# RWKV-7 outputs turned to channels by tokens, with centred values as weights and their squares summed on TensorE

## The chip, the cores and the metric
One core of one Trainium2 chip. The metric is device time in microseconds of one execution of the whole program. The kernel before: 929.25 us, median of 3 runs (929.19 to 930.19). Engines are named as in the profile: PE (TensorE), DVE (VectorE), ACT (ScalarE), POOL (GpSimd), SP (the queue that issues most loads).

## The reference
A two-layer trunk over 256 tokens of width 1024: an RWKV-7 time mix, a SwiGLU block, a shared K/V projection, a dilated window attention and a second SwiGLU block. Only the output of the time mix is touched. Cut to what matters:

```python
o = wkv7_scan(rh, decay, kh, vh, -kk, kk * ah)     # (1, 256, 16 heads, 64), linear in vh
mean = jnp.mean(o, axis=-1, keepdims=True)         # per token and head
var = jnp.mean(jnp.square(o - mean), axis=-1, keepdims=True)
o = (o - mean) * lax.rsqrt(var + LNX_EPS)
o = o.reshape(Bn, Sn, Dn) * lnx_g + lnx_b
bonus = jnp.sum(rh * kh * r_k, axis=-1, keepdims=True) * vh
y = (o + bonus.reshape(Bn, Sn, Dn)) * g            # then y @ w_o, added to x
```

The scan is linear in the values, so values whose mean over the 64 channels of a head has been taken away give outputs whose mean is already zero.

## The kernel before
The time mix runs as four groups (`group(it)`, it 0 to 3) of 256 channels, that is four heads; the program is written out by hand for each engine, with semaphores between them, so that each engine's order is the order of the code. In a group the 256 tokens are two chunks of 128. The stages of a group on PE, in order:

- the head: `second_rank` (two small products), the query projection in four quarters (`project_parts(4, ...)`), `turn_output(it)` (the outputs of the group before are turned by four transposes into bank 2), `sums_of_squares` (squares of the keys), the value projection (`values`) with `turn_norms` (L650 to 654) inside it;
- the matrices (`pe_mats`), with `product_o` of the group before between the chunks;
- six levels `l` of a blocked triangular inverse, small matmuls that alternate with DVE; `values_fill(l)` puts other work of PE between them. At `l == 4` it turns the values `vT` by four transposes (L741) into `Vn`, tokens by channels;
- the state phase (L786 to 848): the last products of the inverse, then for chunk 0 `UUs`, the new state (`pe_S`, bank 2), the output (`pe_o`, bank 3), for chunk 1 `pe_z1`, `UUs`, and the output (bank 6). `next_keys(v)` puts a quarter of the next group's key projection between them; the last group has none, and `keep_clock` multiplies the identity by itself there.

The outputs of a group lie tokens by channels. DVE's `norm_output(it, c)` takes the sum over the 64 channels of a head, subtracts the mean, ACT squares (`square_output`), DVE sums the squares, POOL takes the root (`root`, L2123), DVE scales into `on`. `turn_output` then turns `on`, and `gate_turned` (or `gate_output` at the end) multiplies by the gain and the gate, adds the bonus, and the product with `w_o` follows. `pe_on`, `dve_on`, `dve_oc`, `act_osq`, `pool_ors` are the semaphores of this chain.

After the last group comes a tail (L864 to 870): `product_o(NGRP, [0])`, the turn of chunk 1, `product_o(NGRP, [1], 1, [0])`, `turn_half_rows(0, 0)` (the normalised first token tile of the SwiGLU block, which needs both halves of `product_o` of tile 0 added to x), `product_o(NGRP, [1], 1, [1])`. Most matmuls are recorded at the helper's line L496, transposes at their own line. A matmul of plain float32 shows as two records of weight load and matmul, a transpose as one.

Of the kernel before, what the change touches and what calls it, by code (L numbers as in the profile page):

```python
# [16 lines left out]
ALU = mybir.AluOpType  # L17
# [24 lines left out]
def constants():  # L42
# [4 lines left out]
    out["halves"] = (p // HD == f // HD).astype(np.float32)  # L47
    strict, incl = (p < f), (p <= f)
# [40 lines left out]
def program(nc, ins, out):  # L89
    ctx = ExitStack()  # L90
    with ctx:
# [51 lines left out]
        ident, halves = C("ident"), C("halves")  # L143
# [82 lines left out]
        on = cg.take(512, "p (c n i) -> p c n i", c=2, n=2)  # L226
        yT = cg.take(512, "p (n t) -> p n t", n=2)
# [266 lines left out]
        def _(pe):  # L494
# [135 lines left out]
            def group(it, behind=True, ahead=True):  # L630


                def next_keys(v):
# [6 lines left out]
                    else:  # L640
# [17 lines left out]
                if behind:  # L658
# [3 lines left out]
                    turn_output(it)  # L662
# [46 lines left out]
                def values_fill(l):  # L709
# [112 lines left out]
                pe.wait_ge(S("dve_S"), it + 1)  # L822
                pe.wait_ge(S("pool_M"), it * 2 + 2)
                for n in range(2):
                    mm(bank[4][:, n * P:(n + 1) * P], ar[:, n, 1, 0, :], St[:, n, :], True, False)
                    for h in range(2):
                        u = 2 * n + h
                        m = mm(hcols(bank[4], u), M[:, 4 + u, 2, :], Vn[:, 1, n, h * HD:(h + 1) * HD], False, h == 1)
                m.then_inc(S("pe_z1"), 1)
                next_keys(2)  # L830
# [9 lines left out]
                for n in range(2):  # L840
                    mm(bank[6][:, n * P:(n + 1) * P], ar[:, n, 1, 1, :], St[:, n, :], True, False)
                    for h in range(2):
                        u = 2 * n + h
                        hh = slice(h * HD, (h + 1) * HD)
                        o = hcols(bank[6], u)
                        mm(o, M[:, 4 + u, 3, :], Vn[:, 1, n, hh], False, False)
                        m = mm(o, M[:, 4 + u, 1, :], UUs[:, 1, n, hh], False, h == 1)
                m.then_inc(S("pe_o"), 1)
# [260 lines left out]
        def _(act):  # L1109
# [65 lines left out]
            def square_output(it, c):  # L1175
                act.wait_ge(S("dve_oc"), it * 2 + (c - 1))
                A(osq[:, c * T:(c + 1) * T], oc[:, c * T:(c + 1) * T], ACT.Square).then_inc(S("act_osq"), 1)

            def group(it, behind=True, ahead=True):
# [38 lines left out]
                if behind:  # L1218
                    decays()
                else:  # L1220
# [62 lines left out]
                for c in range(2):  # L1283
                    if c == 1 and not ahead:
                        square_output(NGRP, 0)
                    if c == 1:
                        act.wait_ge(S("pe_z1"), it + 1)
# [6 lines left out]
                if ahead:  # L1294
                    A(small[:, 63:64], onec[:, 0:1], ACT.Sigmoid)
                    square_output(it + 1, 0)
# [4 lines left out]
            square_output(NGRP, 1)  # L1301

# [200 lines left out]
        def _(dve):  # L1503
# [143 lines left out]
            def norm_output(it, c, meanwhile=None, squaring=None):  # L1647

                o = bank[(3, 6)[c]][:, 0:T].rearrange("p (u i) -> p u i", u=4)
                cut = slice(c * T, (c + 1) * T)  # L1650
                st = [gsm[:, 8 * i + 4 * c:8 * i + 4 * c + 4] for i in range(6)]
                dve.wait_ge(S("pe_o"), it * 2 + (c - 1))
# [544 lines left out]
```

## Time and profile before

| | before |
|---|---|
| median of 3 runs | 929.25 us (929.19 to 930.19) |
| the profiled execution's own time | 934.33 us |
| its span | 932.0 us |
| mean granted TensorE clock | 0.993 |
| busy: PE, DVE, ACT, POOL | 920.8, 681.7, 501.8, 101.4 us |
| the time mix in the span | about the first 273 us |

The profiled execution is 5.08 us longer than the median of the runs. Times in the trace count from the start of its span. PE's busy time counts a matmul until its modelled end, so the pace of PE is read from starts, not from busy shares.

### The profile page before, as it was taken

How to read it: one execution, taken by the hardware profiler on the slowest of the kernel's cores; microseconds unless marked ns; L12 is line 12 of the kernel's file. 1: busy time of each engine (PE TensorE's matmuls, PEld its weight loads, DVE VectorE, ACT ScalarE, POOL GpSimd, SP SyncE). 2: the span in 40 equal slices, each digit the busy share in tenths (PEclk: the TensorE clock that was granted, in tenths of full speed). 3: DMA queues.
4: the chain of work that ended last, by engine and by line, in shares of the span. 5: the costliest groups of instructions: out<-in, count | busy, mean ns of one | idle time of the engine just before them, and what ended most of it. 6: DMA issues, size and time to landing. Idle time of an engine off the chain costs nothing.

```text
span 932.0 us, 18317 instructions
## 1 busy us (share of the span) xinstructions
PE 920.8 (99%) x7008; PEld 818.6 (88%) x7008; DVE 681.7 (73%) x1294; ACT 501.8 (54%) x818; POOL 101.4 (11%) x75
## 2 busy tenths in 40 slices
PE   9999999999999999999999999999999999999998
PEld 7789889798879888888899999999998888888887
DVE  7877877778466756666687888889879666666665
ACT  4563544544244545444457776767777445445442
POOL 0211000000012000000041133213222000000000
PEclk9999999999799999999999999999999999999999
DMA  9311213203407676667369545554654256676661
GB/s 298 132 60 46 91 60 105 92 1 107 145 1 202 178 223 178 185 193 217 104 206 292 152 132 163 148 155 139 171 159 114 71 162 186 192 203 195 188 180 45
DMA packets 195241, 136.71 MB, mean 147 GB/s; under 512 B 7390, under 2 KB 186078, under 8 KB 195180
## 3 DMA queue, kind: packets, MB, share of 16 engines
q1 hardware_dynamic: 194748, 135.13, 49.3%
q8 instruction: 44, 0.72, 0.3%
q10 hardware_dynamic: 432, 0.72, 0.3%
q14 instruction: 17, 0.14, 0.1%
HBM read 134.78 MB, written 1.05 MB: 146 GB/s over the span
## 4 chain that ended last, share of the span: by engine, by line
PE 94%; DVE 3%; issue 2%; ACT 1%; POOL 0%; POOLq 0%; DVEq 0%
PE bank L496 52%; PE wide L496 37%; DVE work L1505 1%; PE wide L1029 1%; PE wide L1052 1%; PE bank L1029 1%; PE bank L1052 1%; DVE x L1505 0%; POOL gsm L2123 0%; PE wide L653 0%; PE wide L741 0%; PE wide L787 0%; PE bank L519 0%; ACT work L1111 0%; PE bank L596 0%
## 5 line engine op out<-in xcount | busy, mean ns | idle before, releaser
L496 PE MATMUL bank<-wpj,hkq 128*128 128x384 f32 x1152 | 215.5, 340 | 1.5 <-ACT Vs L1111 0.4
L496 PEld LDWEIGHTS bank<-wpj,hkq 128*128 128x128 f32 x1152 | 197.5, 188 | 6.1 <-issue 4.2
L496 PE MATMUL wide<-hsp,wsp 128*128 128x256 f32 (+2 forms) x1120 | 196.0, 329 | 1.6 <-DVE hsp L1505 1.6
L496 PEld LDWEIGHTS wide<-hsp,wsp 128*128 128x128 f32 x1120 | 172.4, 190 | 24.3 <-DVE hsp L1505 2.4
L1505 DVE TENSOR_TENSOR wsp<-ring,wsp 128x1024 fp32r<-128x1024 f32 (+1 forms) x88 | 150.6, 1752 | 4.2 <-ACT wsp L1111 4.2
L1111 ACT ACTIVATE wsp<-ring 128x1024 fp32r<-128x1024 f32 (+1 forms) x88 | 130.3, 1484 | 26.5 <-DMA ring<-in_f_w_gu 15.6
L2123 POOL TENSOR_TENSOR gsm<-gsm,mhalf 128x6 f32<-128x6 f32 (+1 forms) x40 | 74.3, 1876 | 317.4 <-DVE gsm L2041 174.0
L1111 ACT ACTIVATE rows<-wide 128x256 f32<-128x256 f32 x66 | 25.4, 384 | 145.7 <-PE wide L496 145.7
L496 PE MATMUL bank<-wsp,asp 128*128 128x512 f32 x396 | 98.1, 392 | 0.0
L1505 DVE TENSOR_TENSOR wpj<-ring,wpj 128x1536 fp32r<-128x1536 f32 x48 | 84.1, 1753 | 17.0 <-ACT wpj L1111 17.0
L496 PEld LDWEIGHTS bank<-wsp,asp 128*128 128x128 f32 x396 | 71.8, 189 | 13.1
L1111 ACT ACTIVATE wpj<-ring 128x1536 fp32r<-128x1536 f32 x48 | 71.1, 1485 | 6.6 <-PE bank L496 6.3
L496 PEld LDWEIGHTS bank<-work 64*64 64x64 f32 (+4 forms) x1216 | 58.9, 140 | 16.1 <-issue 6.2
L496 PE MATMUL bank<-work 64*64 64x32 f32 (+7 forms) x1216 | 71.1, 237 | 1.6
L1505 DVE TENSOR_TENSOR am<-sg,rows 128x256 f32<-128x256 f32 x44 | 19.1, 435 | 71.4 <-ACT sg L1111 70.8
L496 PE MATMUL bank<-hsp,wsp 128*128 128x256 f32 (+1 forms) x368 | 68.7, 330 | 0.0
L1111 ACT ACTIVATE work<-wide 128x256 f32<-128x256 f32 (+3 forms) x73 | 30.9, 441 | 67.6 <-PE wide L496 28.6
L496 PE MATMUL wide<-work 64*64 64x32 f32 (+6 forms) x720 | 62.7, 265 | 0.7 <-DVE work L1505 0.4
L496 PEld LDWEIGHTS bank<-hsp,wsp 128*128 128x128 f32 x368 | 56.9, 190 | 6.2
L496 PEld LDWEIGHTS wide<-work 64*64 64x64 f32 (+4 forms) x720 | 54.4, 160 | 4.5 <-issue 1.7
L1505 DVE TENSOR_TENSOR rows<-wide,rows 128x256 f32<-128x256 f32 x66 | 27.9, 424 | 37.3 <-ACT rows L1111 37.3
L496 PE MATMUL wide<-wsp,asp 128*128 128x512 f32 x132 | 37.1, 390 | 0.0
(295 smaller groups left out, 1333.4 us busy)
## 6 DMA issues: line engine op xcount, KB each, us to landing
ring<-in_f_w_gu SPq DMA_DIRECT2D x88, 512.0 KB, 6.0
ring<-in_w_kv SPq DMA_DIRECT2D x96, 256.0 KB, 3.5
ring<-in_f_w_down SPq DMA_DIRECT2D x44, 512.0 KB, 3.7
ring<-in_b_w_q SPq DMA_DIRECT2D x48, 256.0 KB, 3.4
wmix<-in_a_w_k SPq DMA_DIRECT2D x4, 1024.0 KB, 5.2
wmix<-in_a_w_r SPq DMA_DIRECT2D x4, 1024.0 KB, 5.6
wmix<-in_a_w_v SPq DMA_DIRECT2D x4, 1024.0 KB, 5.3
wmix<-in_a_w_o SPq DMA_DIRECT2D x4, 1024.0 KB, 5.0
```

The source lines that it names most:

```text
L496: return pe.matmul(o, a, b, start=start, stop=stop)
L1029: m = pe.transpose(QK[w][r][:, g * P:(g + 1) * P], akr[:, 2 * w + r, g * P:(g + 1) * P], ident)
L1052: m = pe.transpose(SCORES[r][h][:, j * P:(j + 1) * P], pr[r][:, h, j * P:(j + 1) * P], ident)
L1111: return act.activation(o, i, f, **k)
L1505: return dve.tensor_tensor(o, a, b, op)
L2123: return pool.tensor_tensor(dst, src, mhalf[:, 0:n], ALU.pow)
```

## The change
- The outputs are computed channels by tokens. `heads_out` makes four matmuls, for two pairs n and two heads h: the weights are 64 columns of the values (`Vn`), of `UUs` or of the state `St`, 128 tokens of a matrix M or `ar` move, and head h lands in its own 64 partitions of bank 3 or 6. Before, M (128 columns) was the weight and 64 channels moved.
- `vT` is turned by four float32 matmuls with the constant `centre` (identity less 1/64 within a head) instead of by four transposes, so that `Vn` is centred.
- ACT squares the outputs straight from the banks. PE sums the squares of each head with `output_squares` (two matmuls a chunk, two columns moving), in front of `sums_of_squares`. DVE makes the variance for both chunks in one step, POOL takes one root of 8 columns, ACT spreads it (`spread_roots`) into `on`, and `turn_output` turns that into bank 1, now between quarters 1 and 2 of `values`.
- DVE: `norm_output` goes; `gate_heads` multiplies the outputs by gain and gate straight from banks 3 and 6; one multiplication with the turned roots is put ahead of `dve_scaled`.
- The state phase: the products with `Vn` and M are put ahead of the waits for `act_uu` and `dve_S`.
- The last group: `keep_clock` stays for v 0 and 2 alone; the turn of chunk 0 leaves the state phase; the tail is reordered.

The core of the diff:

```diff
+    out["centre"] = out["ident"] - out["halves"] / HD
@@ turn_output, output_squares
-                pe.wait_ge(S("dve_on"), it * 2 + (chunks[-1] - 1))
+                pe.wait_ge(S("act_ors"), it + (chunks[-1] if it == NGRP else 0))
...
+            def output_squares(it, c, b):
+                pe.wait_ge(S("act_osq"), it * 2 + (c - 1))
+                for n in range(2):
+                    m = mm(bank[b][:, 8 + 4 * c + 2 * n:10 + 4 * c + 2 * n], osq[:, c * T + n * P:c * T + (n + 1) * P], halves[:, 0:P:HD])
+                return m
@@ head of a group on PE
-                        keep_clock((4, 4, 4, 3)[v], 7)
+                    elif v in (0, 2):
+                        keep_clock(4, (7, 1)[v // 2])
...
                     pe.wait_ge(S("act_sq"), it + 1)
+                    if behind:
+                        pe.wait_ge(S("dve_oc"), it * 2)
+                        for c in range(2):
+                            output_squares(it, c, 3)
...
-                    turn_output(it)
                     sums_of_squares()
...
-                    values(range(early - 1, 4))
+                    values([early - 1])
                     pe.wait_ge(S("act_sa"), it + 1)
+                    turn_output(it, b=1)
+                    values(range(early, 4))
@@ values_fill, l == 4
-                                m = pe.transpose(bank[6][:, (2 * c + n) * P:(2 * c + n + 1) * P],
-                                                 vT[:, n * T + c * P:n * T + (c + 1) * P], ident)
+                                m = mm(bank[6][:, (2 * c + n) * P:(2 * c + n + 1) * P], vT[:, n * T + c * P:n * T + (c + 1) * P], cent)
@@ state phase
+                def heads_out(b, c, first, weights, moving, last):
+                    for n in range(2):
+                        for h, hh in enumerate(BLK):
+                            m = mm(bank[b][hh, n * P:(n + 1) * P], weights(n, hh), moving(n, 2 * n + h), first and n == 0, last and n == 1)
+                    return m
+                for n in range(2):
+                    mm(bank[2][:, n * P:(n + 1) * P], kPn[:, n, :], Vn[:, 0, n, :], n == 0, False)
+                pe.wait_ge(S("act_U"), it * 2 + 2)
+                heads_out(3, 0, True, lambda n, hh: Vn[:, 0, n, hh], lambda n, u: M[:, u, 3, :], False)
                 pe.wait_ge(S("act_uu"), it * 2 + 1)
                 for n in range(2):
-                    mm(bank[2][:, n * P:(n + 1) * P], kPn[:, n, :], Vn[:, 0, n, :], True, False)
-                    m = mm(bank[2][:, n * P:(n + 1) * P], bPn[:, n, :], UUs[:, 0, n, :], False, True)
+                    m = mm(bank[2][:, n * P:(n + 1) * P], bPn[:, n, :], UUs[:, 0, n, :], False, n == 1)
                 m.then_inc(S("pe_S"), 1)
+                heads_out(3, 0, False, lambda n, hh: UUs[:, 0, n, hh], lambda n, u: M[:, u, 1, :], True).then_inc(S("pe_o"), 1)
+                pe.wait_ge(S("pool_M"), it * 2 + 2)
                 for u in range(4):
-                    hh = slice((u % 2) * HD, (u % 2 + 1) * HD)
-                    mm(hcols(bank[3], u), M[:, u, 3, :], Vn[:, 0, u // 2, hh], True, False)
-                    m = mm(hcols(bank[3], u), M[:, u, 1, :], UUs[:, 0, u // 2, hh], False, True)
-                m.then_inc(S("pe_o"), 1)
+                    mm(hcols(bank[4], u), M[:, 4 + u, 2, :], Vn[:, 1, u // 2, (u % 2) * HD:(u % 2 + 1) * HD], u == 0, False)
...
                 m.then_inc(S("pe_z1"), 1)
+                if not ahead:
+                    output_squares(NGRP, 0, 7).then_inc(S("pe_ss"), 1)
                 next_keys(2)
...
+                heads_out(6, 1, True, lambda n, hh: St[:, n, hh], lambda n, u: ar[:, n, 1, 1, :], False)
+                heads_out(6, 1, False, lambda n, hh: Vn[:, 1, n, hh], lambda n, u: M[:, 4 + u, 3, :], False)
                 next_keys(3)
-                if not ahead:
-                    turn_output(NGRP, [0])
                 pe.wait_ge(S("act_uu"), it * 2 + 2)
...
+                heads_out(6, 1, False, lambda n, hh: UUs[:, 1, n, hh], lambda n, u: M[:, 4 + u, 1, :], True).then_inc(S("pe_o"), 1)
@@ tail on PE
-            product_o(NGRP, [0])
-            keep_clock(1, 4)
+            turn_output(NGRP, [0])
+            keep_clock(2, 4)
+            output_squares(NGRP, 1, 7).then_inc(S("pe_ss"), 1)
+            product_o(NGRP, [0], 0, [0])
+            pe.wait_ge(S("dve_oc"), NGRP * 2 - 1)
             turn_output(NGRP, [1], 3)
-            keep_clock(6, 4)
+            product_o(NGRP, [0], 0, [1])
+            keep_clock(2, 4)
             product_o(NGRP, [1], 1, [0])
@@ ACT
-                act.wait_ge(S("dve_oc"), it * 2 + (c - 1))
-                A(osq[:, c * T:(c + 1) * T], oc[:, c * T:(c + 1) * T], ACT.Square).then_inc(S("act_osq"), 1)
+                act.wait_ge(S("pe_o"), it * 2 + (c - 1))
+                A(osq[:, c * T:(c + 1) * T], bank[(3, 6)[c]][:, 0:T], ACT.Square).then_inc(S("act_osq"), 1)
...
             square_output(NGRP, 1)
+            spread_roots(NGRP, 0, 4)
+            spread_roots(NGRP, 1, 4)
@@ DVE
+            def gate_heads(it, c):
+                dve.wait_ge(S("act_osq"), it * 2 + (c - 1))
+                for n in range(2):
+                    m = stt(oc_nt[:, n, c * P:(c + 1) * P], bank[(3, 6)[c]][:, n * P:(n + 1) * P], pl[:, n, 0:1],
+                            gT[:, n * T + c * P:n * T + (c + 1) * P], ALU.mult, ALU.mult)
+                m.then_inc(S("dve_oc"), 1)
...
+                if behind:
+                    dve.wait_ge(S("pe_on"), it)
+                    dve.wait_ge(S("dve_oc"), it * 2)
+                    q.mark(tt(yT.rearrange("p n t -> p (n t)"), bank[1], oc, ALU.mult))
                 q.sync()
                 tt(flat(bP), bb, En, ALU.mult).then_inc(S("dve_scaled"), 1)
...
-            gate_output(NGRP, 0)
-            norm_output(NGRP, 1, lambda: add_output(NGRP, [0]))
-            add_output(NGRP, [1])
+            gate_heads(NGRP, 1)
+            dve.wait_ge(S("pe_ss"), NGRP + 2)
+            mean_squares_out(bank[7], 1, 4)
+            gate_output(NGRP, 0)
             gate_output(NGRP, 1)
+            add_output(NGRP, [0, 1])
```

## Rows read from the trace of the kernel before

**Rows 1.** The page: busy time by engine, and the granted clock in 40 slices.
```profile
PE 920.8 (99%) x7008; PEld 818.6 (88%) x7008; DVE 681.7 (73%) x1294; ACT 501.8 (54%) x818; POOL 101.4 (11%) x75
PEclk9999999999799999999999999999999999999999
```

**Rows 2.** The chain that ended last, group 2: start, length, engine, line, records.
```profile
151.57 0.44 PE bank L596 x4
...
155.76 0.66 PE wide L653 x4
```

**Rows 3.** Timeline of PE, state phase of group 1: start, us, what, count.
```profile
135.96 1.05 PE L496 MATMUL bank<-work 128*128 128x128 f32 x8
136.85 3.24 PE L496 MATMUL wide<-work 128*128 128x64 f32 x28
...
143.72 2.34 PE L496 MATMUL wide<-work 128*128 128x128 f32 x20
```

**Rows 4.** Groups of PE by form: 12.0 to 15.5 us, then 20.6 to 24.2.
```profile
L496 PE MATMUL bank<-work 128*64 128x256 f32 x16 | 3.7, 383 | 0.0
...
L496 PE MATMUL bank<-work 128*64 128x256 f32 x32 | 3.7, 383 | 0.0
```

**Rows 5.** Timeline of PE, level 4 of group 3: the values turned, then level 5.
```profile
240.33 0.66 PE L741 MATMUL wide<-cst,work 128*128 128x128 f32 x4
240.92 1.27 PE L496 MATMUL bank<-work 32*32 32x32 f32 x48
```

**Rows 6.** Timeline of PE, heads of groups 1 and 2.
```profile
88.00 1.14 PE L496 MATMUL bank<-work,wa 64*128 64x256 f32 x8
...
94.04 0.66 PE L596 MATMUL bank<-cst,work 128*128 128x128 f32 x4 [0.44 <-DVE work L1505]
94.53 1.00 PE L496 MATMUL wide<-cst,work 128*128 128x2 f32 x8
...
146.00 1.14 PE L496 MATMUL bank<-work,wa 64*128 64x256 f32 x8
...
151.85 0.95 PE L496 MATMUL wide<-cst,work 128*128 128x2 f32 x8
152.66 0.36 PE L496 MATMUL wide<-x_hi 128*128 128x256 f32 x1
```

**Rows 7.** Stretches: busy us of PE, PEld, DVE, ACT, POOL, then granted clock.
```profile
70.05:76.47 6.42, 6.28 (x54) 5.80 (x53) 4.01 (x6) 1.29 (x4) 0.00 (x0) 0.73 0.00 0
129.53:134.45 4.92, 4.78 (x54) 4.40 (x53) 4.01 (x6) 1.28 (x4) 0.00 (x0) 1.00 0.01 3
...
244.00:254.55 10.55, 10.55 (x67) 10.21 (x65) 3.49 (x4) 1.67 (x5) 0.00 (x0) 0.52 0.25 73
...
183.50:186.80 3.30, 3.18 (x84) 2.71 (x82) 2.65 (x10) 2.60 (x7) 0.00 (x0) 1.00 0.18 52
240.90:244.30 3.40, 3.28 (x83) 2.96 (x83) 2.78 (x9) 2.89 (x8) 0.00 (x0) 1.00 0.02 5
```

**Rows 8.** Timeline of PE, the tail.
```profile
262.75 3.65 PE L496 MATMUL bank<-wmix,work 128*128 128x512 f32 x8
...
266.75 0.44 PE L596 MATMUL wide<-cst,work 128*128 128x128 f32 x2
...
270.17 1.11 PE L519 MATMUL bank<-cst,fhn 128*128 128x128 f32 x8
```

**Rows 9.** Timelines of DVE, ACT and POOL in the tail.
```profile
267.22 0.61 DVE L1508 SCALAR_TENSOR_TENSOR work<-wide,pl,work 128x128 f32<-128x128 f32 x2
267.87 0.42 DVE L1505 TENSOR_TENSOR work<-work 128x256 f32<-128x256 f32 x1
...
264.07 0.42 ACT L1111 ACTIVATE work<-work 128x256 f32<-128x256 f32 x1 [4.07 <-DVE work L1505]
...
265.22 1.01 POOL L2123 TENSOR_TENSOR gsm<-gsm,mhalf 128x4 f32<-128x4 f32 x1 [5.44 <-DVE gsm L1662]
```

**Rows 10.** Groups of POOL over the whole run: the root of six columns.
```profile
L2123 POOL TENSOR_TENSOR gsm<-gsm,mhalf 128x6 f32<-128x6 f32 x32 | 65.3, 2064 | 174.0 <-DVE gsm L2041 174.0
```

More of the change, by code:

```diff
@@ L141, in C @@
             return cst[:, a:a + n]
-        ident, halves = C("ident"), C("halves")
+        ident, halves, cent = C("ident"), C("halves"), C("centre")
         class Carve:
@@ L820, in group @@
-                m.then_inc(S("pe_o"), 1)
+                    mm(hcols(bank[4], u), M[:, 4 + u, 2, :], Vn[:, 1, u // 2, (u % 2) * HD:(u % 2 + 1) * HD], u == 0, False)
                 pe.wait_ge(S("dve_S"), it + 1)
-                pe.wait_ge(S("pool_M"), it * 2 + 2)
                 for n in range(2):
[L825 to L828, printed above, removed]
+                    m = mm(bank[4][:, n * P:(n + 1) * P], ar[:, n, 1, 0, :], St[:, n, :], False, n == 1)
@@ L1175, in square_output, with spread_roots @@
             def square_output(it, c):
[L1176 to L1177 removed]
+                act.wait_ge(S("pe_o"), it * 2 + (c - 1))
+                A(osq[:, c * T:(c + 1) * T], bank[(3, 6)[c]][:, 0:T], ACT.Square).then_inc(S("act_osq"), 1)
+            def spread_roots(it, c=0, n=8):
+                act.wait_ge(S("pool_ors"), it + c)
+                A(on.rearrange("p c n i -> p (c n i)")[:, c * T:c * T + n * HD].rearrange("p (u i) -> p u i", u=n),
+                  gsm[:, 40 + 4 * c:40 + 4 * c + n].rearrange("p (u o) -> p u o", o=1).broadcast_to([P, n, HD]), ACT.Copy).then_inc(S("act_ors"), 1)
             def group(it, behind=True, ahead=True):
@@ L1283, in group @@
                 for c in range(2):
-                    if c == 1 and not ahead:
-                        square_output(NGRP, 0)
                     if c == 1:
+                        square_output(it + 1, 0)
                         act.wait_ge(S("pe_z1"), it + 1)
@@ L1645, in gu_lo @@
                 low_part(wsp[:, 1 - b, 1, 0:2048], raw[b][:, 0:2048], wsp[:, 1 - b, 0, 0:2048], "dve_gu_lo")
[L1647 to L1652, printed above, removed]
-                step(dve.tensor_reduce(st[1], o, AX.X, ALU.add))
-                step(dve.tensor_scalar(st[2], st[1], 1.0 / HD, None, ALU.mult))
-                wide_ = [st[i].rearrange("p (u o) -> p u o", o=1).broadcast_to([P, 4, HD]) for i in (2, 5)]
-                occ = oc[:, cut].rearrange("p (u i) -> p u i", u=4)
-                tt(occ, o, wide_[0], ALU.subtract).then_inc(S("dve_oc"), 1)
-                if squaring:
-                    squaring()
-                dve.wait_ge(S("act_osq"), it * 2 + (c - 1))
-                step(dve.tensor_reduce(st[3], osq[:, cut].rearrange("p (u i) -> p u i", u=4), AX.X, ALU.add))
-                dve.tensor_scalar(st[4], st[3], 1.0 / HD, LNX_EPS, ALU.mult, ALU.add).then_inc(S("dve_var"), 1)
-                if meanwhile:
-                    meanwhile()
-                dve.wait_ge(S("pool_ors"), it * 2 + (c - 1))
-                tt(on[:, c, :, :].rearrange("p n (h i) -> p (n h) i", h=2), occ, wide_[1], ALU.mult).then_inc(S("dve_on"), 1)
@@ new lines, in mean_squares_out, with gate_output @@
+            def mean_squares_out(b, c, n):
+                dve.tensor_scalar(gsm[:, 32 + 4 * c:32 + 4 * c + n], b[:, 8 + 4 * c:8 + 4 * c + n], 1.0 / HD, LNX_EPS,
+                                  ALU.mult, ALU.add).then_inc(S("dve_var"), 1)
+            def gate_output(it, c):
+                cut = slice(c * P, (c + 1) * P)
+                dve.wait_ge(S("pe_on"), it + c)
+                dve.wait_ge(S("dve_oc"), it * 2 + (c - 1))
+                y, bo, turned = yT[:, :, cut], *(v.rearrange("p (n t) -> p n t", n=2)[:, :, cut] for v in (bv, bank[(2, 3)[c]]))
+                step(tt(y, turned, oc_nt[:, :, cut], ALU.mult))
@@ L1808, in group @@
                     receptances()
+                if behind:
+                    dve.wait_ge(S("pe_on"), it)
+                    dve.wait_ge(S("dve_oc"), it * 2)
+                    q.mark(tt(yT.rearrange("p n t -> p (n t)"), bank[1], oc, ALU.mult))
                 q.sync()
@@ L1898, in group @@
                 m.then_inc(S("dve_S"), 1)
-                norm_output(it + 1, 0, None if behind else lambda: low_half("ow", 1), low_values if ahead else None)
+                if ahead:
+                    low_values()
+                gate_heads(it + 1, 0)
+                if ahead and not behind:
+                    low_half("ow", 1)
+                if not ahead:
+                    dve.wait_ge(S("pe_ss"), NGRP + 1)
+                    mean_squares_out(bank[7], 0, 4)
             group(0, behind=False)
@@ L2143, in _ @@
                     pool.affine_select(M[:, us, 2:4, :], M[:, us, 2:4, :], [[0, 4], [1, 2], [1, P]], ALU.is_ge, 0.0, base=-1, channel_multiplier=-1).then_inc(S("pool_M"), 1)
-                for c in range(2):
-                    pool.wait_ge(S("dve_var"), it * 2 + (c + 1))
-                    root(gsm[:, 40 + 4 * c:44 + 4 * c], gsm[:, 32 + 4 * c:36 + 4 * c], 4).then_inc(S("pool_ors"), 1)
+                for c in range(1 if it < NGRP - 1 else 2):
+                    pool.wait_ge(S("dve_var"), it + c + 1)
+                    n = 8 if it < NGRP - 1 else 4
+                    root(gsm[:, 40 + 4 * c:40 + 4 * c + n], gsm[:, 32 + 4 * c:32 + 4 * c + n], n).then_inc(S("pool_ors"), 1)
             norm_root(1)
```

32 lines of the change are left out of this document (5 added, 27 removed).

## The prediction

> **What bounds the kernel now.** I read the page first, then the chain of waits, then PE's timeline around each edited place, then the clock by stretches. The page has PE busy all the time, and its clock strip shows one slice of 40 below full [rows 1]. In the chain of waits over groups 1 to 3 almost every step is PE; the turn of the outputs, which waits for DVE, ACT and POOL, stands there as PE work with no wait ahead of it in group 2, and so does the turn of the norms [rows 2]. So until the end of the last group PE's own record count, its pace and its clock set the time, and what DVE saves (two reductions, three small steps and a gate) is worth nothing by itself. Two places differ. In group 1 PE stands idle at the turn for DVE [rows 6]. In the tail the chain leaves PE: the last outputs pass DVE, ACT, DVE, POOL and DVE before PE can turn them 4.00 us after it made them (262.75 to 266.75), with product and identity work put between [rows 8]. There waits are the bound.
>
> **Price of a record.** State products: eight records start from 135.96 to 136.85, 0.89/8 = 0.111 us each, though 128 columns move; the next 28 move 64 columns for 3.1 us, again 0.11 each [rows 3]. So with 128 columns as weights the load sets the pace, not what moves. Column halves: 16 records of 64-column weights with 256 moving take 3.7 us when all go to one half, and 32 take the same 3.7 us when they alternate between the halves [rows 4]. Two halves run side by side. `heads_out` alternates in the same way with 128 moving, so I take 0.11 us for a pair and 4 x 0.11 = 0.44 us for a call of eight records. From both sides: 0.89 us if nothing overlaps, 0.44 if all does; I take 0.44, since the nearest row has exactly this alternation.
>
> The change of array shape has a price too. Four transposes with full weights start at 240.33, and the next, smaller shape starts at 240.92 [rows 5]: 0.59 us, less 4 x 0.11, is 0.15 for a switch. Bounds 0.09 to 0.2; I take 0.15.
>
> **The Trainium skill speaks against this step.** Rows 4 have the overlap. "TensorE: Matmul & The Clock Gate", section "The mechanism", says that a weight load overlaps a running matmul only where the row groups differ; here all tiles have all rows. By that rule each pair would also wait for its loads. The rows disagree, since 32 loads beside 32 matmuls add nothing to 16; the sum goes by the rows.
>
> **State phase of a group, chunk 0.** Before: 8 + 28 = 36 records x 0.11 = 4.0 us [rows 3]. After: the state 8, M with Vn 8 and ar with St 4 are 20 records, 2.2 us; two calls of `heads_out` 0.9; four switches 0.6. Sum 3.7, so -0.3. Chunk 1: before 20 records, 2.3 us (143.72 to 146.00) [rows 3, 6]; after three calls 1.3 and three more switches 0.45, so -0.5. Together -0.8 a group in groups 0 to 2. The value products ahead of the waits gain nothing there, for a quarter of the next keys already stands in front of each wait. The new wait for `act_U` stands behind it too, and ACT's copy needs 0.4 us.
>
> **Level 4.** The transposes are four records, four float32 matmuls eight: +4 x 0.11 = +0.44 in each of four groups. The next level starts as soon as PE is free [rows 5], so all of it counts.
>
> **Head of groups 1 to 3.** Two calls of `output_squares` are eight more records in front of the norms' sums. The same eight for the keys take 151.85 to 152.66, +0.81 [rows 6]; the turn moves into the values and breaks their stream once more, +0.1. Sum +0.9. Group 1 gives its wait back: from the start of the group to the squares it needs 94.53 - 88.00 = 6.53 us, group 2 151.85 - 146.00 = 5.85 [rows 6], so -0.68; DVE's two gates and ACT's square are done long before. New waits: PE waits for `act_ors` with quarters 2 and 3 of the values, the matrices and all else queued behind it. POOL's root has eight columns; four took 1.01 us [rows 9], six 2.06 on average [rows 10], so 1 to 3 us. PE reaches the new turn late: after the sums (152.66) [rows 6] it projects until the turn of the norms (155.76) [rows 2], turns them (0.44) and makes a quarter of the values (12 records of 0.12, 1.4), 4.9 us in all. DVE's two steps, POOL's 1 to 3 and ACT's spreading (0.6) fit, so I cost it at nothing; a root of 4 us would cost 0.5 us a group. `dve_scaled` comes one multiplication later on DVE, which has lost two gates of the same width ahead of it, and PE comes 0.9 later as well. Nothing.
>
> **Last group.** Head and level 4: +0.9 + 0.44. State phase at full clock from the first `pe_uu` to the last output: before 36 + 20 + 8 (the second UUs) + 22 of `keep_clock` = 86 records, 9.5, and the turn with its wait 0.4: 9.9. After: 3.7, squares 0.44, `keep_clock` 0.9, UUs 0.9, chunk 1 1.55: 7.5. So -2.4.
>
> **Tail.** From the last output (before: 262.75) to `turn_half_rows` (270.17) it is 7.42 us [rows 8]. After, in order: ACT's square 0.2 + 0.42; only then, since ACT's order is so, the roots of chunk 0 are spread, 0.4; PE turns them at 1.05, then identity and squares until 2.2. DVE makes the variance until 2.6 and then the output of chunk 0 in two steps of 0.42 [rows 9], to 3.5. Only now can `product_o` start, which before started at 0 and filled the chain. Its half takes four records of 0.43 (eight took 3.65) [rows 8], to 5.2, the turn of chunk 1 and the other half to 7.25. That half must be added to x, squared, rooted and scaled before `turn_half_rows`; before, that took from 266.2 (262.75 and eight records) to 270.17 [rows 8], 3.9 us, a part of it in DVE's queue; I take 3.6, so 10.9. PE is done with the rest at 9.4 and waits. 10.9 - 7.4 = +3.5 us; bounds +2.5 (steps overlap better) to +4.5. POOL's 1.0 us root [rows 9] is hidden behind the product.
>
> **Sum without the clock.** Group 0: -0.8 + 0.44 = -0.3 (rounded down); group 1: -0.8 + 0.44 + 0.9 - 0.7 = -0.1; group 2: +0.6; group 3: +1.3 - 2.4 = -1.1; tail +3.5. Together +2.6 us.
>
> **The clock.** The granted clock falls to half in group 0 and in group 3, each time right behind levels 4 and 5, a stretch of small matmuls with few full-array ones; in groups 1 and 2 the same stretch is followed by full clock [rows 7]. The same work takes 6.42 us in group 0 and 4.92 in group 1: 1.5 us lost. Were all of it work of PE at its clock, 6.42 us at 0.73 would lose 6.42 x 0.27 = 1.7, so the loss is 0.87 of that figure. In group 3 the stretch from 244.00 to 254.55 ran at 0.52 [rows 7]: 10.55 x 0.48 x 0.87 = 4.4 lost. Together 5.9 us (bounds 1.5, if group 3's stretch waits as much as it works, and 6.8). The change doubles the full-array records in just this stretch (level 4) and packs the state phase more densely, so I expect neither fall.
>
> **Sum.** 934.33 (the profiled execution) + 2.6 - 5.9 = 931.0. The median lies 5.1 below that execution; I carry the difference, 929.25 - 3.3 = 925.9, and move to 926.5, since some of those 5.1 us may be falls that the timed runs didn't have.
>
> **Rivals.**
> 1. The tail decides (slower). The timed runs lose little to the clock, or the denser stretch isn't enough and the clock falls in group 3 or in the tail's new gaps (PE has work for less than half of its first 3.5 us) as before. Then the +2.6 stands, less 0 to 1 of identity work that is dropped at half clock: 929.25 + 2.6 = 931.9. It decides as soon as the clock gives back less than 2.6 - 1.9 = 0.7 us. For it: the 5.1 us between profile and runs. Against it: two falls in four groups are in the trace.
> 2. Half of it: the fall of group 0 goes (its level 4 gains most), that of group 3 stays: 929.25 + 2.6 - 1.5 - 0.9 (identity work dropped at half clock counts double) = 929.4. No change.
> 3. The column halves don't run side by side with 128 moving, or loads aren't hidden: up to 5 x 0.45 a group, four groups, +9: about 935.5. Against it: rows 4.
> 4. The change doesn't do what it says, PE isn't relieved in the state phase because DVE's state (`dve_S`) comes last: DVE may still be subtracting weights when `pe_S` is there. It would eat the 0.8 a group, +2.4 in all: about 929. Against it: PE has 1.5 us of products in between, and DVE's two steps are like the 0.61 of [rows 9].
>
> **Chances.** Forecast (926.5, 924 to 927.4) 0.47; rival 1 0.25; rivals 2 and 4 0.20; rival 3 0.04; better than 924 (both the clock and a shorter tail) 0.04. A difference of 0.2%, 1.9 us, is about what a measurement of this kernel can tell from no change. Faster by more: 0.50; within: 0.22; slower by more: 0.28. The range 923.5 to 932.5 leaves out rival 3 and half of the outer ends. The likeliest case's own range is 924 to 927.4.
>
> **What would show it.** In the profile after: `heads_out` eight records in 0.44 us plus a switch; level 4 eight records; the head of group 1 with no idle time; the granted clock at 1.00 after level 5 in groups 0 and 3; PE idle in the tail at about 2 to 3.5 us and again ahead of the transposes of `turn_half_rows`, 10.9 us after the last output. I am wrong if the clock still falls in group 3, or if that last distance is near 7.4.

## The result, and the profile after

| | before | after |
|---|---|---|
| median | 929.09 us of 8 runs (928.33 to 930.31) | 933.42 us of 8 runs (930.71 to 935.05) |
| ratio | | 1.004, interval 1.0025 to 1.0055 |
| profiled execution | 934.33 us, span 932.0, clock 0.993 | 932.56 us, span 930.8, clock 0.998 |

The change makes the kernel 4.3 us slower in these runs (3.2 over all runs below). The forecast was 926.5, with a range up to 932.5: wrong in its sign, and outside its range. The two profiled executions taken alone say the opposite, 1.8 us faster, and that contradiction is where the error sits.

The page of after, busy time and the clock strip, against [rows 1]:

```profile
PE 917.0 (99%) x7052; PEld 810.7 (87%) x7052; DVE 670.0 (72%) x1262; ACT 504.6 (54%) x823; POOL 99.5 (11%) x72
PEclk9999999999999999999999999999999999999999
```

The page counts 44 matmuls more (7052 against 7008), and DVE is 12 us less busy, which is worth nothing, as PE sets the pace. The slice below full clock is gone from the strip. The stretches of after, with the columns of [rows 7], show what is behind a slice of 23 us:

```profile
70.00:74.50 4.50, 4.50 (x33) 4.11 (x33) 2.58 (x5) 1.36 (x4) 0.00 (x0) 0.67 0.00 0
244.00:254.60 10.60, 10.31 (x136) 9.12 (x133) 6.76 (x15) 4.10 (x12) 0.00 (x0) 1.00 0.15 43
```

The clock is at its lower level for a part of group 0 still (0.67 over 4.5 us), and full in group 3, where it was 0.52 before. In the timeline of PE, level 4 of group 3, then group 1's state phase, then the head of group 2, against [rows 3, 5 and 6]:

```profile
242.26 1.16 PE L498 MATMUL wide<-cst,work 128*128 128x128 f32 x8
243.35 1.27 PE L498 MATMUL bank<-work 32*32 32x32 f32 x48
...
136.94 0.61 PE L498 MATMUL bank<-work 128*128 128x128 f32 x4
137.48 0.66 PE L498 MATMUL wide<-work 128*64 128x128 f32 x8
138.06 0.71 PE L498 MATMUL bank<-work 128*128 128x128 f32 x4
138.71 2.19 PE L498 MATMUL wide<-work 128*64 128x128 f32 x20
...
146.32 1.14 PE L498 MATMUL bank<-work,wa 64*128 64x256 f32 x8
...
151.76 1.84 PE L498 MATMUL wide<-cst,work 128*128 128x2 f32 x16
...
156.56 0.66 PE L666 MATMUL wide<-cst,work 128*128 128x128 f32 x4
```

Level 4 takes 1.09 us from start to start, before 0.59. `heads_out` is the form 128\*64: eight records and a switch of shape in 0.58 us (137.48 to 138.06). The turn of the norms (L666) stands 10.24 us behind the start of group 2, before 155.76 - 146.00 = 9.76. The state phase, from the first state product to the start of the next group, takes 146.32 - 136.94 = 9.38 us, before 146.00 - 135.96 = 10.04 [rows 3, 6]. The tail, all engines; a bracket is idle time and what ended it:

```profile
258.54 0.38 ACT L1127 ACTIVATE work<-wide 128x256 f32<-128x256 f32 x1 [1.09 <-PE wide L498]
...
258.95 0.42 ACT L1127 ACTIVATE work<-gsm 128x256 f32<-128x256 f32 x1
...
259.42 0.44 PE L598 MATMUL bank<-cst,work 128*128 128x128 f32 x2 [0.93 <-ACT work L1127]
...
260.14 0.51 PE L498 MATMUL bank<-cst,work 128*128 128x2 f32 x4
...
260.69 0.16 DVE L1679 TENSOR_SCALAR gsm<-bank 128x4 f32<-128x4 f32 x1 [1.12 <-PE bank L498]
260.77 0.42 DVE L1527 TENSOR_TENSOR work<-bank,work 128x256 f32<-128x256 f32 x1
...
261.23 0.42 DVE L1527 TENSOR_TENSOR work<-work 128x256 f32<-128x256 f32 x1
...
261.70 1.98 PE L498 MATMUL bank<-wmix,work 128*128 128x512 f32 x4 [1.05 <-DVE work L1527]
...
268.90 1.31 PE L521 MATMUL bank<-cst,fhn 128*128 128x128 f32 x8 [1.12 <-DVE fhn L1530]
```

The last output is read by ACT at 258.54. PE waits for ACT's spread roots (0.93), for DVE's output of chunk 0 (1.05), and for the normed x (1.12), and `turn_half_rows` (L521) starts 10.4 us behind the last output; before it was 7.42 [rows 8].

### The profile page after: what moved, and what is told of

Same layout as the page of the kernel before. It is cut to its first block, busy times and chain, and to the rows that moved or that the text cites. A ratio compares the mean times of both kernels' runs of the same rounds, so it can differ in the third digit from the quotient of the medians.

```text
span 930.8 us, 18381 instructions
## 1 busy us (share of the span) xinstructions
PE 917.0 (99%) x7052; PEld 810.7 (87%) x7052; DVE 670.0 (72%) x1262; ACT 504.6 (54%) x823; POOL 99.5 (11%) x72
## 3 DMA queue, kind: packets, MB, share of 16 engines
HBM read 134.85 MB, written 1.05 MB: 146 GB/s over the span
## 4 chain that ended last, share of the span: by engine, by line
PE 95%; DVE 3%; issue 2%; ACT 0%; POOL 0%; POOLq 0%; DVEq 0%
PE bank L498 52%; PE wide L498 38%; DVE work L1527 1%; PE wide L1045 1%; PE bank L1045 1%; PE wide L1068 1%; PE bank L1068 1%; DVE x L1527 0%; PE bank L521 0%; PE wide L666 0%; PE wide L800 0%; PE bank L598 0%; PE wide L737 0%; ACT squared L1127 0%; DVE fhn L1530 0%
## 5 line engine op out<-in xcount | busy, mean ns | idle before, releaser
L498 PEld LDWEIGHTS wide<-hsp,wsp 128*128 128x128 f32 x1120 | 172.4, 190 | 24.2 <-DVE hsp L1527 2.3
L2141 POOL TENSOR_TENSOR gsm<-gsm,mhalf 128x6 f32<-128x6 f32 (+2 forms) x37 | 72.5, 1981 | 326.6 <-DVE gsm L2059 174.1
L1127 ACT ACTIVATE work<-wide 128x256 f32<-128x256 f32 (+3 forms) x81 | 34.0, 435 | 73.8 <-PE wide L498 44.7
L498 PEld LDWEIGHTS bank<-work 64*64 64x64 f32 (+4 forms) x1216 | 56.4, 136 | 16.7 <-issue 6.0
L498 PE MATMUL wide<-work 64*64 64x32 f32 (+6 forms) x736 | 57.8, 266 | 0.7 <-DVE work L1527 0.4
L498 PEld LDWEIGHTS wide<-work 64*64 64x64 f32 (+5 forms) x736 | 45.9, 147 | 6.9 <-issue 2.4
```

What stands on the lines that cost most here:

```text
L498: return pe.matmul(o, a, b, start=start, stop=stop)
L1127: return act.activation(o, i, f, **k)
L2141: return pool.tensor_tensor(dst, src, mhalf[:, 0:n], ALU.pow)
```

## Two theories and the experiments

Theory A: the work is longer by about what was summed (+2.6), and the clock that the profile of before lost was mostly that one execution's, so that there was next to nothing to give back. Theory B: the work costs nothing, and the timed runs of after are slow by the clock. To tell them apart, each timed run is read with its mean granted clock. The table has all runs of this study (in "before", the runs beside every experiment too; the eight of the result have no clocks listed and are not in it; three single runs of 2299 to 4887 us, one of before, one of after and one of `b_ahead`, are left out; the medians quoted with a ratio count them). The experiments were run in four sets, on four chips, each with runs of before beside it. At 1.000 before takes 928.6 to 929.0 us on average in the four, so a difference of up to 0.5 us between kernels of different sets says nothing.

| kernel | median | runs at 1.000: mean (count) | runs at 0.997 to 0.999 | runs at 0.996 and below |
|---|---|---|---|---|
| before | 929.3 | 928.9 (73) | 930.1 (33) | 934.2 (13) |
| after | 932.5 | 931.2 (4) | 932.2 (7) | 934.8 (7) |
| `b_lev4` | 931.9 | 931.3 (5) | 932.0 (5) | 935.6 (2) |
| `b_ahead` | 928.6 | 928.5 (7) | 930.2 (2) | 934.3 (2) |
| `a_nosq` | 929.7 | 928.5 (5) | 930.0 (4) | 932.8 (3) |
| `a_serial` | 932.5 | 931.5 (4) | 932.9 (2) | 935.4 (2) |
| `a_keep` | 931.1 | 931.0 (8) | 933.1 (2) | 936.4 (1) |
| `tail` | 930.1 | 929.8 (6) | 931.0 (6) | none |
| `tail2` | 930.9 | 930.7 (7) | 932.1 (3) | 935.6 (1) |
| `tail3` | 930.6 | 930.5 (7) | 931.7 (4) | 934.8 (1) |
| `tail4` | 929.9 | 930.0 (8) | 929.4 (4) | none |

**`b0`, the kernel before again.**

> The kernel before once more, as the one under test, so that the granted clock of each of its runs is listed. Theory A (the changed kernel issues more work, and the clock that the profile of before lost was mostly that one execution's): median 929 us, nearly all runs with a clock of 0.999 or 1.000, and the few with less longer by what the clock lost; the changed kernel at clock 1.000 took 930.7, so at least 1.5 us of its 4.3 are work. Theory B (the change costs nothing but clock): the runs of before at full clock are near 930.5 as well, and its median is lower only because it falls less often.

Median 929.71, ratio 0.9993 (0.9975 to 1.0011). Seven of 12 runs were at 1.000 and took 928.9 on average, one was at 0.993 and took 934.2. Theory A had expected nearly all runs at 0.999 or above, and missed in that: four were at 0.998. The profile of `b0` has full clock throughout, so it is before without its two falls. Its timeline of PE: the first small products on the rows, the second ranks that open groups 0 to 3, the first product of the tail, `turn_half_rows`, and the first product of the FFN:

```profile
7.84 0.66 PE L527 MATMUL bank<-cst,rows 14*128 14x14 f32 x8
...
48.63 1.14 PE L496 MATMUL wide<-work 64*128 64x256 f32 x8
...
87.00 1.14 PE L496 MATMUL bank<-work,wa 64*128 64x256 f32 x8
...
144.92 1.13 PE L496 MATMUL bank<-work,wa 64*128 64x256 f32 x8
...
202.10 1.13 PE L496 MATMUL bank<-work,wa 64*128 64x256 f32 x8
...
257.35 3.65 PE L496 MATMUL bank<-wmix,work 128*128 128x512 f32 x8
...
264.77 1.11 PE L519 MATMUL bank<-cst,fhn 128*128 128x128 f32 x8
...
267.38 3.14 PE L496 MATMUL wide<-hsp,wsp 128*128 128x256 f32 x24
```

The two ends of the same distance in the profiled before:

```profile
7.36 0.66 PE L527 MATMUL bank<-cst,rows 14*128 14x14 f32 x8
...
272.78 2.42 PE L496 MATMUL wide<-hsp,wsp 128*128 128x256 f32 x18
```

The span of `b0` is 926.5, that of the profiled before 932.0. From the first small products on the rows to the first product of the FFN `b0` takes 259.54 us, before 265.42: the falls did cost 5.9 us in that execution. By [rows 7] the fall in group 0 takes 6.42 x 0.27 / 932 = 0.0019 off an execution's mean clock and that in group 3 10.55 x 0.48 / 932 = 0.0054, so an execution with both is at 0.993. Of the 119 runs of before 12 are at 0.993 or 0.994. Theory A holds on this point, theory B's claim on full-clock runs (930.5) doesn't: before and after differ by 2.3 us at full clock.

**`a1`, the changed kernel again.**

> The changed kernel once more, for the clocks of its runs. So far: 930.7 at clock 1.000 (one run), 932.5 at 0.998, 934.6 at 0.996, against 929.0, 930.1 and none for before. Theory A (work and clock both): at equal clock 1.7 to 2.4 us above before; and fewer than half of the runs at 1.000 (of before: 28 of 47), so that the median lies another 1 to 2 us higher. Rival: the first eight runs were unlucky, most runs now are at 1.000, and the median is about 930.8.

Median 932.37, ratio 1.0035 (1.002 to 1.0049). Theory A holds, the rival falls: three of the ten runs are at 1.000. Four of all 18 runs of after are at 1.000, against 73 of 119 of before. So the work isn't all: over all runs the mean is 932.98 - 929.79 = 3.2 us apart, 2.3 of it at full clock, 0.9 from more falls. The profile of `a1`, at 0.996, has two falls, and shows where. Stretches, columns as in [rows 7]:

```profile
70.00:74.50 4.50, 4.50 (x32) 4.11 (x31) 2.41 (x5) 1.16 (x4) 0.00 (x0) 0.62 0.00 0
...
259.00:266.00 7.00, 5.59 (x18) 3.21 (x19) 2.09 (x7) 2.51 (x3) 1.01 (x1) 0.76 0.00 0
```

The timeline of PE in the second of them:

```profile
261.64 3.20 PE L498 MATMUL bank<-wmix,work 128*128 128x512 f32 x4 [1.05 <-DVE work L1527]
```

The second fall is in the tail, behind the waits that the change brought there: four products take 3.20 us, in the profile after 1.98. The profile of `a_serial` (below) has a fall at the same place, and the one of `tail3` in group 2, again right behind levels 4 and 5, where neither before nor after lost any clock. A row of the timeline of `a_serial`, then a stretch of `tail3`:

```profile
259.89 3.68 PE L498 MATMUL bank<-wmix,work 128*128 128x512 f32 x4 [1.05 <-DVE work L1527]
...
187.00:192.00 5.00, 4.95 (x44) 4.58 (x43) 2.61 (x5) 0.52 (x2) 0.00 (x0) 0.67 0.00 0
```

**`a_keep`, the tail's gaps filled.**

```
+            keep_clock(4, 4)
             turn_output(NGRP, [0])
             keep_clock(2, 4)
             output_squares(NGRP, 1, 7).then_inc(S("pe_ss"), 1)
+            keep_clock(4, 4)
...
             product_o(NGRP, [1], 1, [0])
+            keep_clock(5, 4)
             turn_half_rows(0, 0)
```

> The changed kernel with 13 more identity products in the three gaps of its tail where PE waits (0.9 us ahead of the turn of chunk 0, 1.05 us ahead of product_o, 1.1 us ahead of turn_half_rows); they fit in the gaps, so at clock 1.000 the time should be the same 930.7. Theory A (the tail's gaps are what makes the clock fall more often): no run at 0.996 or below, median 1 to 2 us under the changed kernel's. Rival (the falls come from elsewhere, the level and state phases): the same spread of clocks as the changed kernel, the same median.

Median 931.12, ratio 1.0029 (1.0014 to 1.0044). At 1.000 it takes the same as after (931.0 and 931.2), but 8 of 11 runs are there, against 4 of 18. One run at 0.995 remains, where theory A expected none, so not all falls came from the tail. The counts speak against the rival (same spread), but don't shut it out: of the runs of after in the same set, 3 of 10 were at 1.000, and identity products in the tail can't mend a fall in group 0. A fall in the tail is seen in the profiles of `a1` and `a_serial`, and in none of `a_keep` and of the `tail` versions. So that the gaps bring falls and filling them takes these away is likely, not shown. Its profile is after at full clock, and stands beside `b0` row for row:

```profile
47.90 1.13 PE L498 MATMUL wide<-work 64*128 64x256 f32 x8
...
86.12 1.13 PE L498 MATMUL bank<-work,wa 64*128 64x256 f32 x8
...
144.05 1.13 PE L498 MATMUL bank<-work,wa 64*128 64x256 f32 x8
...
201.98 1.14 PE L498 MATMUL bank<-work,wa 64*128 64x256 f32 x8
...
256.29 1.16 PE L498 MATMUL wide<-cst 128*128 128x128 f32 x8
...
266.76 1.32 PE L521 MATMUL bank<-cst,fhn 128*128 128x128 f32 x8
```

| stretch | `b0` | `a_keep` | difference | forecast |
|---|---|---|---|---|
| group 0 | 38.37 | 38.22 | -0.15 | -0.3 |
| group 1 | 57.92 | 57.93 | 0.0 | -0.1 |
| group 2 | 57.18 | 57.93 | +0.75 | +0.6 |
| group 3 up to the last output | 55.25 | 54.31 | -0.9 | -1.1 |
| last output to `turn_half_rows` | 7.42 | 10.47 | +3.05 | +3.5 |
| sum | 216.14 | 218.86 | +2.7 | +2.6 |

The last output is taken where the next work starts: in `a_keep` the identity products at 256.29, in `b0` the product at 257.35. The group's stretch runs to there, the tail's from there to L521 and L519.

**`b_lev4`, level 4 alone.**

```
-                                m = pe.transpose(bank[6][...], vT[...], ident)
+                                m = mm(bank[6][...], vT[...], ident)
```

> The kernel before with one part of the change alone: the four turns of the values at level 4 are float32 matmuls against the identity, eight records in place of four. Theory A: PE has no slack there, so +0.44 us in each of four groups, +1.8 us at equal clock. Rival: DVE or ACT come last in that stretch and it costs nothing; or the additional full-array records keep the clock up and it is 1 to 4 us faster than before.

Median 931.93, ratio 1.0021 (1.0003 to 1.004). The groups of its profile (full clock) are 0.46, 0.55 and 0.51 us longer than those of `b0`, and the stretch from the start of group 3 to the FFN 0.51: +2.0 where 1.8 was expected. At 1.000 the runs give +2.4. Nothing in the stretch hides it, and the additional full-array records don't keep the clock up: 7 of 12 runs are below 1.000, of before 46 of 119.

**`a_nosq`, the heads without the output's squares.**

```
-                        for c in range(2):
-                            output_squares(it, c, 3)
+                        pe.wait_ge(S("act_osq"), it * 2)
...
-                        mean_squares_out(bank[3], 0, 8)
+                        dve.tensor_scalar(gsm[:, 32:40], bank[3][:, 0:8], 1.0 / HD, LNX_EPS, ...)
```

> The changed kernel without the sums of the output's squares in the heads of groups 1 to 3 (their eight records left out; the variance is taken from the sums of the keys' squares, so what is computed differs there). Theory A: 0.8 to 0.9 us less in each of three groups, -2.5 us from the changed kernel at equal clock, about 931. Rival: turn_output then waits for POOL's root instead, and less than 1 us comes back.

Median 929.72; at 1.000 it takes 928.5, 2.7 us less than after. Its groups 1 and 2 take 57.06 and 57.04 us, 0.87 and 0.89 less than in `a_keep`: eight records of 0.11. `turn_output` doesn't wait for POOL in them. The term of the head is shown.

**`b_ahead`, the value products ahead of the waits alone.**

```
+                for n in range(2):
+                    mm(bank[2][...], kPn[:, n, :], Vn[:, 0, n, :], n == 0, False)
+                pe.wait_ge(S("act_U"), it * 2 + 2)
+                heads(3, 0, Vn, 3, True, False)
                 pe.wait_ge(S("act_uu"), it * 2 + 1)
...
+                heads(4, 1, Vn, 2, True, False)
                 pe.wait_ge(S("dve_S"), it + 1)
...
```

> The kernel before with one part of the change alone: in the state phase the products with the values stand ahead of the waits for UU and for the state, with the operands as they were (same records, same count). Theory A (a quarter of the next keys already stands in front of each wait, so PE never waits there): 0 in groups 0 to 2, less than 0.3 us in group 3; 929.0 at clock 1.000. Rival (PE waits for the state and for UU unseen): 0.5 to 2 us less.

Median 928.95, ratio 1.0007 (0.9989 to 1.0025). Its groups 0 to 2 take 38.37, 57.96 and 57.17 us, those of `b0` 38.37, 57.92 and 57.18. From the start of group 3 to the FFN it takes 65.44 us, `b0` 65.28, so nothing is gained there either. So this part of the change is worth nothing, as was said; what the state phase gains comes from the column halves. The runs at 1.000 are 0.4 us under before's, no more than the sets differ from each other.

**`a_serial`, the column halves one after the other.**

```
-                    for n in range(2):
-                        for h, hh in enumerate(BLK):
+                    for h, hh in enumerate(BLK):
+                        for n in range(2):
```

> The changed kernel with one edit: heads_out goes through the two column halves one after the other instead of in alternation; the records are the same. Theory A (the halves run side by side only when neighbouring records use different ones, as the forecast took it): eight records take 0.8 to 0.9 us in place of 0.44, five calls in each of four groups, +7 to +9 us: about 939. Rival (a record of 64 columns of weights is cheap in itself, side by side or not): the same time as the changed kernel, 931 at clock 1.000.

Median 932.51, ratio 1.0038 (1.0024 to 1.0052), at 1.000 931.5. Theory A as I had put it falls: the alternation isn't what gives the overlap. Its timeline of PE, group 1:

```profile
135.49 0.67 PE L498 MATMUL wide<-work 128*64 128x128 f32 x8
136.09 0.71 PE L498 MATMUL bank<-work 128*128 128x128 f32 x4
```

Eight records and the switch take 0.60 us (135.49 to 136.09), alternating 0.58. The groups are 0.09 us longer, not 2. The rival's reading, that such a record is cheap in itself, isn't shown by that: see the last section.

**`tail`, chunk 0 of the last group finished early.**

```
                 next_keys(3)
+                if not ahead:
+                    turn_output(NGRP, [0])
...
-            turn_output(NGRP, [0])
             keep_clock(2, 4)
...
+            spread_roots(NGRP, 0, 4)
             square_output(NGRP, 1)
-            spread_roots(NGRP, 0, 4)
...
+            gate_output(NGRP, 0)
             gate_heads(NGRP, 1)
             dve.wait_ge(S("pe_ss"), NGRP + 2)
             mean_squares_out(bank[7], 1, 4)
-            gate_output(NGRP, 0)
```

> The changed kernel with one thing put back: in the last group the roots of chunk 0 are spread, turned and multiplied ahead of the last output, not behind it, so that product_o can start some 0.7 us after the last output instead of 3.3 us. Theory A (the tail is the largest term, +3 us): 2.6 us less than the changed kernel, about 930.8 at equal clock, and 1 to 2 us above before. Theory B (the clock is the cause): the same 933.4, or less than 1 us better, since PE's records are the same in number.

Median 930.12, ratio 0.9997 (0.998 to 1.0014): not told from before by the median. At 1.000 it takes 929.8, 0.9 more than before and 1.4 less than after, where 2.6 was expected; and none of 12 runs is at 0.996 or below. `product_o` starts 1.7 us sooner (its distance from the start of group 3 is 55.69, in after 57.43), but behind the squares of chunk 1, and `turn_half_rows` 1.7 us sooner than in `a_keep`.

**`tail2` and `tail3`, the product ahead of the squares.** `tail2` differs from `tail` in PE's order and in the number of identity products in the gaps; `tail3` also spreads chunk 0's roots ahead of the copy of UU and adds to x ahead of the output of chunk 1.

```
             keep_clock(2, 4)
-            output_squares(NGRP, 1, 7).then_inc(S("pe_ss"), 1)
             product_o(NGRP, [0], 0, [0])
+            output_squares(NGRP, 1, 7).then_inc(S("pe_ss"), 1)
+            product_o(NGRP, [0], 0, [1])
             pe.wait_ge(S("dve_oc"), NGRP * 2 - 1)
             turn_output(NGRP, [1], 3)
-            product_o(NGRP, [0], 0, [1])
...
```

> As the kernel `tail`, with the first half of product_o ahead of the squares of chunk 1, since there the product waited for the squares (260.0) though its input was ready at 259.35. Theory A (the end of product_o for the first rows sets turn_half_rows): 0.4 us less than `tail` at equal clock, about 929.3 at 1.000, level with before. Rival (chunk 1's root, which now comes 1.7 us later, takes its place): the same as `tail` or up to 0.5 us more.

> As `tail2`, and the two things that still came late there are moved: ACT spreads chunk 0's roots ahead of its copy of UU, and DVE adds product_o's first rows to x ahead of the output of chunk 1, for whose turn it waited in `tail2`. Theory A (the order of the queues in the tail, not the number of steps, makes it longer): from product_o's first product to turn_half_rows 7.6 us (before 7.4, `tail2` 9.2), 1.3 us less than `tail2` at equal clock, about 929.8 at 1.000; the rest above before is group 2's and 3's head (+0.75 each). Rival (chunk 1's chain squares, root, spread, turn, gate is longer than that of before and sets the end): no gain, 930.7 at 1.000.

Medians 930.9 and 930.6, at 1.000 930.7 and 930.5: both slower than `tail` (0.7 us or more at 1.000), and neither gives what was expected. The timeline of `tail3`, ACT and DVE:

```profile
262.77 0.42 ACT L1128 ACTIVATE work<-gsm 128x256 f32<-128x256 f32 x1 [3.60 <-POOL gsm L2143]
...
263.09 1.90 ACT L1128 ACTIVATE wsp<-ring 128x2048 fp32r<-128x2048 f32 x1
...
263.31 0.69 DVE L1529 TENSOR_TENSOR x<-bank,x 128x512 f32<-128x512 f32 x1 [1.06 <-PE bank L498]
...
264.89 0.61 ACT L1128 ACTIVATE squared<-x 128x512 f32<-128x512 f32 x1
```

x is ready at 264.0, but ACT squares it at 264.89: the squares of chunk 1 come later on PE, so do POOL's root and ACT's spread, and behind the spread ACT's queue holds a copy of FFN weights of 1.90 us, which now falls into the chain.

**`tail4`, the squares first again.**

> The kernel `tail3` with the squares of chunk 1 ahead of product_o again. In `tail3` their place behind the first half of product_o made chunk 1's root 1.3 us later, and ACT, which works in its order, spread it at 262.77 and copied 1.9 us of FFN weights (263.09 to 265) before it could square x, for which DVE was ready at 264.0. Theory A (ACT's queue is what made `tail2` and `tail3` lose): from product_o's first product to turn_half_rows 7.4 us again (`tail` 7.43, `tail3` 8.87), turn_half_rows 1.2 to 1.5 us earlier than in `tail3`, 929.2 to 929.6 at clock 1.000, still 0.4 to 1 us above before. Rival (product_o's late half or the output of chunk 1 sets it): no more than 0.5 us less than `tail3`.

Its PE order is that of `tail`, with `tail3`'s early spread, and DVE adds the first half to x ahead of chunk 1's output. Median 929.9, ratio 1.0 (0.9986 to 1.0013). From `product_o` to `turn_half_rows` it is 7.42 us again, `tail3` 8.87, which bears the reading of ACT's queue out. The FFN starts 65.84 us behind the start of group 3, in `tail` 65.85, so the earlier spread is worth nothing. At 1.000 it takes 930.0, above the range that was expected: behind the start of the FFN its profile is 0.9 us longer than those of `b0`, `a_keep` and `tail` (660.15 against 659.1 to 659.3), which isn't explained. No version of the changed kernel beats before.

## Why the prediction was wrong, point by point

- **What bounds the kernel**: right. DVE's 12 us are worth nothing, PE's records and the tail's waits set the time.
- **State phase**: -0.8 a group forecast, -0.66 measured (10.04 to 9.38), so it was a little oversized. Group 2 agrees, where +0.75 is 0.50 (level 4) and 0.9 (squares and the moved turn) less 0.66. Its cause was half right. The 0.44 us for a call stands (0.58 with its switch), but not because of the alternation, as `a_serial` shows. That the value parts gain nothing ahead of the waits was right (`b_ahead`).
- **The rule against this step**: the loads hide, as the sum had it. Full-array records take 0.10 to 0.11 us each whether 128 columns move ([rows 3]) or two ([rows 6]), so moving 128 columns hides behind the loads, though all records use all rows. The Trainium skill, "TensorE: Matmul & The Clock Gate", section "The mechanism", has a line by which the loads would hide only where the row groups differ, and the rows disagree with it; the prediction left out that the same section also lets a load run ahead into a background weight buffer, and with that the rows agree.
- **Level 4** was a little undersized: 0.44 forecast, 0.46 to 0.55 measured. The two switches of shape around it were there before.
- **Head**: 0.9 forecast, 0.87 to 0.89 for the records (`a_nosq`). Group 1's idle wait came back as forecast: its difference is 0.75 less than group 2's, where 0.68 stood in the sum. The new waits cost nothing; PE shows no idle time at `turn_output` in the groups, and POOL's root of eight columns took 1.7 us, within the 1 to 3 that were allowed.
- **Last group**: -1.1 forecast, -0.9 measured. The forecast took 1.55 us for chunk 1 there and 1.75 (1.3 and 0.45) in the other groups, which is a slip of 0.2.
- **Tail**: +3.5 forecast, +3.05 measured, in the order of events that the text gives. This is the largest term.
- **Sum without the clock**: +2.6 forecast (2.5 without its rounding), +2.7 in the two traces at full clock, +2.3 in the timed runs at full clock. That it comes so near is in part luck: the tail came out 0.45 lower, the groups together 0.6 higher.
- **The clock: this is the step that failed.** The 5.9 us were well sized (265.42 against 259.54 in `b0`; the spans, 932.0 and 926.5, differ by 5.5, since `b0` starts 0.5 later), but two things were wrong with how they were used. First, they were the loss of one execution, and the step "Sum" carried nearly all of them over to the median: "I carry the difference". The median run of before has no fall (73 of 119 at 1.000), so there was nothing to give back; over all runs of before the clock costs 929.8 - 928.9 = 0.9 us on average, not 5.9. The 5.1 us between the profiled execution and the median said just that, and stood in the text only as "some of those 5.1 us may be falls that the timed runs didn't have"; nearly all of them were. Second, "I expect neither fall" was wrong: the one in group 0 is in the profiles of after, `a1` and `tail`, and the waits of the tail bring a new place for them. Rival 1 named both, put the result at 931.9, and should have been the forecast. It still missed 1.5 us of the first median: only one of those eight runs is at 1.000, four are at 0.996 or below. Neither of the two signs that the prediction gave for being wrong came up (group 3 of after ran at full clock, and the last distance is 10.4), since they tested the sum and the profile, not the step from the profile to the median.
- Why group 3 falls in some executions of before and not in others isn't settled. Whether the denser stretch saves it in after isn't either. None of the nine profiles of the changed kernel and its variants has that fall, and none of their 96 timed runs is below 0.995, while 12 of 119 of before are: the pair of falls of the profiled before wasn't seen again after the change. But five of the 96 are at 0.995, which fits group 3's fall alone as well as three short ones.

## What to carry to other kernels

A loss seen in one profiled execution belongs to the median only if the profiled time equals the median; here the profile was 5.1 us above it, and that was the clock loss (5.9) to within 1 us. Price it by runs: list each run's granted clock beside its time and compare runs of equal clock. Moving work from an engine off the critical path to the one on it costs its full price (0.11 us a record, 2.7 us here for the 24 records of squares in the heads) plus, in a serial tail, every hand-over that can't be covered any more; and PE's new waits there can cost a second time through its clock, as in `a1` and `a_serial`.

## What the runs showed of the hardware

- Records with 64 columns of weights and 128 moving go at 0.055 us each, whether neighbours use different column halves or four in a row use the same (0.58 and 0.60 us for eight with the switch). I had expected 0.11 for the second. In the trace of `a_serial` the matmuls of a call start in pairs 13 ns apart, the later pairs 0.11 us behind each other. One half alone goes at 3.7/16 = 0.23 us a record with 256 columns moving [rows 4], which by proportion is 0.115 with 128: the distance of the pairs, and not half of it. So a record doesn't look short in itself, though no row has one half alone with 128 moving. The likeliest reading is that the second half's records start beside the first half's although they come later in the program; the trace doesn't name the half of a record, so this is argued, not shown.
- Repeated executions of one unchanged program sort themselves by granted clock: before takes 928.9 us at 1.000, 930.1 at 0.997 to 0.999, and 934.2 below. That is 1.2 us more in the middle class, whose clock fits one short fall (the profiles of after and `tail3`, at 0.998, have one), and 5.3 in the last, whose 0.993 fits the two of [rows 7]. Short falls were seen in group 0, in group 2 and in the tail.
- The start varies too: the first small products on the loaded rows begin between 6.84 us (`tail2`) and 7.97 us (after) into the span, so stages must be compared by distances, not by their place in the span.
